# A transformer layer and a gated block on one core: x loaded first, joined sums, other places for small work, and products of ones in three waits

## The reference

```python
p = rms_norm(x, norm_mix) @ w_in                        # 2048 -> all inputs of the two groups
y = concat(rwkv7_group(p_rwkv), dsa_group(p_att))
h = x + y @ w_mix_out
h = h + memory_cross_attention(rms_norm(h, norm_cross), rms_norm(mem, norm_mem), w_q, w_kv, w_o)
h = h + square(relu(rms_norm(h, norm_mlp) @ w_up)) @ w_down
h = rms_norm(h, norm_final)
m = silu(c) @ ada_w + ada_b                             # six rows of 2048
n = rmsnorm(h, norm_g[0]) * (1 + m[1]) + m[0]
z = gelu(n @ a_w_in); u, v = split(z)
h = h + m[2] * ((u * (w_s @ rmsnorm(v, a_g_v) + b_s)) @ a_w_out)
n = rmsnorm(h, norm_g[1]) * (1 + m[4]) + m[3]
g, v = split(dwconv(n @ ffn_w_up))                      # width 3, along the tokens
h = h + m[5] * ((silu(g) * v) @ ffn_w_down)
out = rmsnorm(h, final_g)
```

## Time and profile before

| | us |
|---|---|
| median of 3 runs | 2686.19 (2685.34 to 2686.24) |
| the profiled execution | 2688.38 |
| its span | 2686.5 |
| PE busy | 2634.9 (98%) |
| PEld busy | 2265.3 (84%) |
| DVE busy | 1930.2 (72%) |
| ACT busy | 1388.5 (52%) |
| POOL busy | 128.0 (5%) |
| DMA | 576.28 MB, mean 215 GB/s |

### The profile page before, as it was taken

The page is one execution under the profiler, slowest core; times in us unless marked ns, Lnnn a source line. Parts: engine busy times, 40 slices in busy tenths (PEclk is TensorE's granted clock), DMA queues, the critical chain, the costliest instruction groups (busy, mean ns, idle before and its releaser), DMA issues.

```text
span 2686.5 us, 45958 instructions
## 1 busy us (share of the span) xinstructions
PE 2634.9 (98%) x16884; PEld 2265.3 (84%) x16884; DVE 1930.2 (72%) x2944; ACT 1388.5 (52%) x2156; POOL 128.0 (5%) x142
## 2 busy tenths in 40 slices
PE   9999998999999999999999999999999999999998
PEld 8888887888888888888878888888788888888886
DVE  5677676777787877878887666578777756775675
ACT  5455565666544544535555454445465535553553
POOL 4500001311000000000000000000000000000000
PEclk8999999999999999999999999999999999999999
DMA  6555201655788888887768855588665565556554
GB/s 220 185 180 176 87 4 66 209 193 171 273 291 287 282 296 276 292 285 277 282 241 323 297 181 170 189 271 281 240 196 188 188 196 188 188 193 191 188 188 149
DMA packets 158110, 576.28 MB, mean 215 GB/s; under 512 B 17856, under 2 KB 18400, under 8 KB 157152
## 3 DMA queue, kind: packets, MB, share of 16 engines
q1 hardware_dynamic: 154784, 562.40, 61.6%
q10 hardware_dynamic: 2512, 10.65, 1.1%
q0 software_dynamic: 624, 0.59, 0.1%
HBM read 570.72 MB, written 2.10 MB: 213 GB/s over the span
## 4 chain that ended last, share of the span: by engine, by line
PE 89%; DVE 5%; POOL 3%; ACT 1%; issue 1%; DMA 1%; ACTq 0%; SPq 0%; DVEq 0%; POOLq 0%
PE ps L2566 31%; PE ps L2570 16%; PE ps L2645 12%; PE ps L2646 12%; PE ps L2647 12%; DVE wlo L2170 2%; PE ps L1091 1%; DMA raw<-in_stream 1%; POOL tab L301 1%; PE ps L1731 1%; POOL ssm L1816 1%; POOL tp L302 0%; ACT whi L1836 0%; PE ps L1104 0%; PE ps L2737 0%
## 5 line engine op out<-in xcount | busy, mean ns | idle before, releaser
L2170 DVE TENSOR_TENSOR wlo<-raw,whi 128x1024 fp32r<-128x1024 f32 x872 | 1057.5, 1228 | 540.9 <-ACT whi L1836 537.7
L1836 ACT ACTIVATE whi<-raw 128x1024 fp32r<-128x1024 f32 x872 | 906.0, 1057 | 806.1 <-PE ps L2570 392.1
L2566 PE MATMUL ps<-xn,whi 128*128 128x512 f32 x3760 | 945.0, 393 | 4.4 <-issue 2.0
L2566 PEld LDWEIGHTS ps<-xn,whi 128*128 128x128 f32 x3760 | 676.6, 189 | 126.2 <-issue 3.9
L2570 PEld LDWEIGHTS ps<-xn,wlo 128*128 128x128 f32 x3760 | 511.6, 191 | 37.1
L2570 PE MATMUL ps<-xn,wlo 128*128 128x256 f32 x3760 | 521.2, 282 | 0.0
L2645 PE MATMUL ps<-whi,act_in 128*128 128x512 f32 x1120 | 436.1, 389 | 0.0
L2646 PE MATMUL ps<-wlo,act_in 128*128 128x512 f32 x1120 | 435.8, 389 | 0.0
L2647 PE MATMUL ps<-whi,act_in 128*128 128x512 f32 x1120 | 435.7, 389 | 0.0
L2645 PEld LDWEIGHTS ps<-whi,act_in 128*128 128x128 f32 x1120 | 210.3, 188 | 44.7 <-DVE wlo L2170 1.0
L2647 PEld LDWEIGHTS ps<-whi,act_in 128*128 128x128 f32 x1120 | 210.3, 188 | 43.6
(11 more groups left out here) (336 smaller groups left out, 2226.8 us busy)
## 6 DMA issues: line engine op xcount, KB each, us to landing
raw<-in_stream SPq DMA_DIRECT2D x872, 512.0 KB, 4.2
adaw<-in_ada SPq DMA_DIRECT2D x96, 512.0 KB, 5.7
adaq<-in_ada SPq DMA_DIRECT2D x96, 512.0 KB, 5.3
h<-in_xT SPq DMA_DIRECT2D x4, 512.0 KB, 7.6
memx<-in_memT ACTq DMA_DIRECT2D x1, 2048.0 KB, 9.3
out<-fin SPq DMA_DIRECT2D x4, 512.0 KB, 4.0
lwa<-in_lora ACTq DMA_DIRECT2D x2, 512.0 KB, 5.0
lwa<-in_lora ACTq DMA_DIRECT2D x1, 1024.0 KB, 7.4
```

Of the source, the lines that this page charges most:

```text
L1836: act.activation(whi[:, r, :], raw[:, r, :], ACT.Copy).then_inc(hi_done, 1)
L2170: dve.tensor_tensor(wlo[:, r, :], raw[:, r, :], whi[:, r, :].bitcast(F32), ALU.subtract)\
L2566: return pe.matmul(ps[:, lin.bank(g, t), :], whi[:, (p0 + s) % RING, c * 512 + t * P:c * 512 + (t + 1) * P], x[:, 2 * s + c, :], start=s + ...
```

## The change

1. Beginning. SP issues x alone, in five pieces, waits for the third of them, and then issues ident, slot 0, par, slots 1 to 3 and the masks, all on its own queue. ACT makes 11 squares and DVE 5; DVE adds two squares each, so that PE sums 8 pairs. PE runs products of ones (`warm`) ahead of the sums (12), behind the second, fourth and sixth (3 each), behind the last (5) and behind the spread of the norm's factor (7). DVE makes both halves of chunks 0 and 1 before it splits slot 0.
2. POOL makes tables 2 and 3 first; ACT takes those at step 28, and 0 and 1 at step 36.
3. `spread_k_t` stands at slot 3 of group 10 instead of slot 2, with `key_d`, `decay_sum_d` and `decays_a` one step later. The sum for memory's norm stands at slot 3 instead of 2. In o, all four parts of the activations stand before the split of slot 2. In mlp the norm's sum is cut over slots 4, 5 and 6, and the transposes of h stand one slot later, ACT's copies one step earlier.
4. Token norms. `base_sums` adds three of the four quarters before the last one is there, so the chain has one step less. The last sum of the modulation of the stage (127, 191) stands before the last residual instead of behind the norm's preparation. At g0 and g1 PE runs 13 (10) products of ones when its last group is done and 5 after the root's input is there; chunks 4 to 7 are transposed behind slot 0's products instead of before them in part.
5. End. Six pieces instead of four; the first ones have 512 columns.

The diff, cut to its core (semaphores and one table of counts are left out):

```diff
--- before.py
+++ after.py
@@ -205,7 +205,7 @@
...
-    IA = Steps([sem("index_a")], "s0 s1 s2 s3 rl0 rl1 rl2 rl3 rl4 rl5 rl6 rl7 vt")
+    IA = Steps([sem("index_a")], "s2 s3 s0 s1 rl0 rl1 rl2 rl3 rl4 rl5 rl6 rl7 vt")
@@ -291,7 +291,7 @@
...
-        for q in range(4):
+        for q in (2, 3, 0, 1):
@@ -518,9 +518,9 @@
...
-        if n == 28:
-            act.wait_ge(tab_p, 1 + 4 * 12)
-            for q in range(4):
+        if n in (28, 36):
+            act.wait_ge(tab_p, 1 + 12 * (2 if n == 28 else 4))
+            for q in (2, 3) if n == 28 else (0, 1):
@@ -538,7 +538,7 @@
...
-        if n == 87:
+        if n == 88:
@@ -613,7 +613,7 @@
...
-        if n == 86:
+        if n == 87:
@@ -714,7 +714,7 @@
...
-        if (g, s) == (10, 2):
+        if (g, s) == (10, 3):
@@ -1515,13 +1517,15 @@
...
+    LAST_SUM = {"mlp": ADA_MLP - 1, "a_uo": ADA_MLP + 2 * ADA_V - 1}
+    OUT = [(0, 0, 512, 0), (1, 0, 512, 1), (0, 512, 512, 0), (0, 1024, 1024, 0), (1, 512, 1024, 1), (1, 1536, 512, 0)]
...
-    PIECE_AT = {0: (0, 1), 1: (2,), 5: (3,), 9: (4,)}
+    PIECE_AT = {0: (0, 1), 2: (2,), 5: (3,), 9: (4,)}
@@ -1737,8 +1741,10 @@
...
-        for q in range(4):
-            sp.dma_start(h[:, 4 * q:4 * q + 4, :], A["xT"][:, 4 * q:4 * q + 4, :]).then_inc(x_in[q], 16)
+        for q, (a, b) in enumerate(((0, 4), (4, 8), (8, 12), (12, 14), (14, 16))):
+            sp.dma_start(h[:, a:b, :], A["xT"][:, a:b, :]).then_inc(x_in[q], 16)
+        sp.wait_ge(x_in[2], 16)
+        sp.dma_start(ident[:, :], A["const"][:, C_ID, :]).then_inc(const_in, 16)
@@ -1756,6 +1762,11 @@
...
+        load(0, 0)
+        sp.dma_start(par[:, :], A["par"]).then_inc(par_in, 16)
+        for r in range(1, 4):
+            load(r, r)
+        mixer["loads"](sp)
@@ -1781,11 +1792,10 @@
...
-        for q in range(2):
-            for b in range(2):
-                sp.wait_ge(scaled_d if b == 0 else scaled_a, 10 + q + 1)
-                sp.dma_start(out[b, :, q * 1024:(q + 1) * 1024], fin[:, b, q * 1024:(q + 1) * 1024]).then_inc(out_in, 16)
-        sp.wait_ge(out_in, 64)
+        for k, (b, c, n, e) in enumerate(OUT):
+            sp.wait_ge(scaled_d if e == 0 else scaled_a, 10 + sum(x[3] == e for x in OUT[:k]) + 1)
+            sp.dma_start(out[b, :, c:c + n], fin[:, b, c:c + n]).then_inc(out_in, 16)
+        sp.wait_ge(out_in, 16 * len(OUT))
@@ -1803,7 +1813,7 @@
...
-                pool.sem_inc(ss_done, 1)
+                pool.sem_inc(ss_done, 16)
@@ -1823,9 +1833,6 @@
...
-        act.dma_start(par[:, :], A["par"]).then_inc(par_in, 16)
-        act.dma_start(ident[:, :], A["const"][:, C_ID, :]).then_inc(const_in, 16)
-        mixer["loads"](act)
@@ -1935,12 +1942,20 @@
...
+            buf = (tt, hl)[q % 2]
...
-            squares(h, tt, 0, range(4 * q, 4 * q + 4))
+            if q >= 2:
+                act.wait_ge(xsum_t, 2 * q - 2)
+            for t in (0, 1, 2) if q < 3 else (0, 2):
+                if q == 3 and t == 2:
+                    act.wait_ge(x_in[4], 16)
+                act.activation(buf[:, t, :], h[:, 4 * q + t, :], ACT.Square).then_inc(xsq_a, 1)
+        act.sem_inc(sq_done, 16)
+        norm("mix")
...
-        norm("mix")
+        prepare("mix", chunks=range(2))
...
-        prepare("mix", ahead=split(L["w_in"]))
+        prepare("mix", chunks=range(2, DC), ahead=split(L["w_in"]))
@@ -2024,10 +2039,9 @@
...
-        cross_high(act, 0)
+        for k in range(4):
+            cross_high(act, k)
...
-        for k in range(1, 4):
-            cross_high(act, k)
@@ -2060,7 +2074,7 @@
...
-                if isinstance(i, int) and (i, p) == (0, 8 * k + 17):
+                if isinstance(i, int) and (i, p) == (0, 8 * k + 16):
@@ -2200,6 +2215,8 @@
...
+                last = lambda k: sst[:, k, :, 3]
+                dve.wait_ge(based, {"final": 3, "g1": 5, "out": 7}[nm])
@@ -2214,18 +2231,16 @@
...
-                total = nt[:, 2:2 + n, :]
-                link(dve.tensor_reduce(total, sst[:, 0:n, :, :], AX_X, ALU.add))
-                x = total[:, 0, :]
+                ins = dve.scalar_tensor_tensor(nt[:, 0, :], last(0), -0.5 / D, sbase[:, 0, :], ALU.mult, ALU.add)
...
-            ins = dve.tensor_scalar(half_x if n == 1 else nt[:, 0, :], x, -0.5 / D, -0.5 * eps, ALU.mult, ALU.add)
+                ins = dve.tensor_scalar(half_x, x, -0.5 / D, -0.5 * eps, ALU.mult, ALU.add)
...
-                link(dve.tensor_scalar(nt[:, 6, :], total[:, 1, :], -0.5 / D, None, ALU.mult))
+                link(dve.scalar_tensor_tensor(nt[:, 6, :], last(1), -0.5 / D, sbase[:, 1, :], ALU.mult, ALU.add))
@@ -2239,7 +2254,7 @@
...
-        def prepare(nm, src, gain, shift=None, chunks=range(DC), ahead=None):
+        def prepare(nm, src, gain, shift=None, chunks=range(DC), ahead=None, at_once=False):
@@ -2256,11 +2271,13 @@
...
-                if j:
+                if at_once:
+                    low(j)
+                elif j and (nm != "mix" or j > 2):
...
-            if j == DC - 1:
+            if j == DC - 1 and not at_once:
@@ -2282,7 +2299,9 @@
...
-                if j:
+                if j == 0:
+                    low(0)
+                elif j > 1:
@@ -2300,11 +2319,26 @@
...
+        def base_sums(nm):
+
+            of = HS[nm][1] if nm != "mlp" else "final"
+            n, eps, k = (2, EPS_1, 0) if of == "final" else (1, EPS_2, 3 if of == "g1" else 5)
+            dve.wait_ge(sqt_done, SQT[of] - (4 if of == "final" else 2))
+            dve.tensor_reduce(sbase[:, 0:n, :], sst[:, 0:n, :, 0:3], AX_X, ALU.add).then_inc(based, 1)
+            dve.wait_ge(based, k + 1)
+            dve.tensor_scalar(sbase[:, 0, :], sbase[:, 0, :], -0.5 / D, -0.5 * eps, ALU.mult, ALU.add).then_inc(based, 1)
+            if n == 2:
+                dve.tensor_scalar(sbase[:, 1, :], sbase[:, 1, :], -0.5 / D, None, ALU.mult).then_inc(based, 1)
+
...
+            if sums_h(nm, i) and (q, b) == (3, 0):
+                base_sums(nm)
+                if nm in LAST_SUM:
+                    sum_ada(LAST_SUM[nm])
@@ -2344,11 +2378,27 @@
...
+            buf = (tt, hl)[q % 2]
...
+            for k, t in enumerate((1, 3) if q == 3 else (3,)):
+                if q == 3 and t == 3:
+                    dve.wait_ge(x_in[4], 16)
+                dve.tensor_tensor(buf[:, t, :], h[:, 4 * q + t, :], h[:, 4 * q + t, :], ALU.mult).then_inc(xsq_d, 1)
+                if q == 3:
+                    dve.wait_ge(xsq_d, 4 + k)
+                    dve.wait_ge(xsq_a, 10 + k)
+                    dve.tensor_tensor(buf[:, 2 * k, :], buf[:, 2 * k, :], buf[:, t, :], ALU.add).then_inc(xsum_d, 1)
+            if q < 3:
+                for k in range(2):
+                    dve.wait_ge(xsq_a, 3 * q + 2 + k)
+                    dve.wait_ge(xsq_d, q + 1)
+                    dve.tensor_tensor(buf[:, 2 * k, :], buf[:, 2 * k, :], buf[:, 2 * k + 1, :], ALU.add).then_inc(xsum_d, 1)
+        norm("mix", EPS_1)
...
-        norm("mix", EPS_1)
+        prepare("mix", h, lambda j: col("norm_mix", j), chunks=range(1), at_once=True)
+        prepare("mix", h, lambda j: col("norm_mix", j), chunks=range(1, 2), at_once=True)
...
-        prepare("mix", h, lambda j: col("norm_mix", j), ahead=split(L["w_in"]))
+        prepare("mix", h, lambda j: col("norm_mix", j), chunks=range(2, DC), ahead=split(L["w_in"]))
@@ -2400,10 +2450,9 @@
...
-        cross_low(dve, 0)
+        for k in range(4):
+            cross_low(dve, k)
...
-        for k in range(1, 4):
-            cross_low(dve, k)
@@ -2465,12 +2514,11 @@
...
-        sum_ada(ADA_MLP - 1)
...
-            elif i < 1:
+            elif i == 1:
@@ -2507,7 +2555,6 @@
...
-        sum_ada(ADA_MLP + 2 * ADA_V - 1)
@@ -2677,6 +2725,9 @@
...
+        def turns_before(s):
+            return () if s == 0 else range(4, 8) if s == 1 else (2 * s + 4, 2 * s + 5)
+
@@ -2729,16 +2783,28 @@
...
-        for _ in range(20):
-            pe.matmul(ps[:, stat_bank["mix"] + 2, 0:P], ones[:, :], ones[:, :], start=True, stop=True)
-        for j in range(DC):
-            pe.wait_ge(sq_done, j + 1)
+        def warm(n, bank=stat_bank["mix"] + 2):
+            for _ in range(n):
+                pe.matmul(ps[:, bank, 0:P], ones[:, :], ones[:, :], start=True, stop=True)
+
+        def warm_until(count, lin, before, behind):
+            pe.wait_ge(evac_done, 8 + 4 * (lin.g0 - 1))
+            warm(before, lin.bank(0, 3))
+            pe.wait_ge(rt_done, count)
+            warm(behind, lin.bank(0, 3))
+        warm(12)
+        for k in range(8):
+            pe.wait_ge(xsum_d, k + 1)
+            x = (tt, hl)[k // 2 % 2][:, 2 * (k % 2), :]
...
-                ins = pe.matmul(ps[:, stat_bank["mix"] + c, 0:1], tt[:, j % 4, c * P:(c + 1) * P], ones[:, 0:1],
-                                start=j == 0, stop=j == DC - 1)
-            ins.then_inc(stat_done if j == DC - 1 else ss_done, 1)
+                ins = pe.matmul(ps[:, stat_bank["mix"] + c, 0:1], x[:, c * P:(c + 1) * P], ones[:, 0:1], start=k == 0, stop=k == 7)
```

(21 more changed lines are left out.)

37 lines of the change are left out of this document (22 added, 15 removed).

## The result

| | before | after |
|---|---|---|
| median of 5 runs, us | 2686.19 (2684.93 to 2688.72) | 2670.38 (2666.97 to 2672.16) |
| profiled execution | 2688.38 | 2670.38 |
| its span | 2686.5 | 2668.6 |

The ratio is 0.9938 with a 95% interval of 0.9926 to 0.995: 16.7 us less, 13.4 to 19.9. Forecast were 2667.7, in a range of 2663 to 2677.5, and 18.5 us less. The medians are 15.8 us apart, the two profiled executions 18.0, their spans 17.9. The forecast was made against the profiled execution of before, which was 2.2 us above its median; the one of after is its median.

A forecast was written before the change was run, and what follows sets the result against it. TensorE (PE), busy 98% of the span, was taken as the bound, so only its pauses and slow stretches count. 6.2+6.5+2.6+0.7+2.0+0.5 = 18.5 us off 2688.38 gives 2669.9, lowered by 2.2 to 2667.7; range 2663 to 2677.5.

The forecast's parts named there:

- Beginning: Start of the kernel: x alone first and halved sums bring the first chunks and slots sooner; 6.2 us.
- Then PE sets the pace: Beginning: once x has landed, PE's sums and fills decide when the sum ends, at 11.6 instead of 17.23.
- The bound of 0.6: Beginning: the gain left, 0.6 us, if fills ran at 0.213 and x came at the first 5 us' rate.
- Five places: Tables, spread_k_t, memory norm's sum, o and mlp's transposes: single waits of PE removed; 6.5 us, bounds 0 and 6.5.
- Norm final and g0: Final norm before g0: fills keep the clock and transposes start slots sooner, 2.6 us; SP's stream 0.7; together 3.3.
- g1: Norm at g1: the same as at g0 with 10 and 5 fills; 2.0 us.
- The term for SP: Behind g0: sum 127 made before the norm frees SP's load stream, so two waits for wlo go; 0.7 us.
- End: Writes at the end: one link less (0.2) and a half-size first write issued 0.35 sooner; 0.5 us.
- so the end follows the first issue: End: writes run without a gap at 404 GB/s, so an earlier first issue brings an earlier end.
- The third rival: Slower: PE's clock in the mixer stays at 0.50 longer; 24 us of such work gives 2691.7; chance 0.03.
- Small waits that come back elsewhere: First rival: weights come later than PE wants, so waits return; 12 us gained, 2674.2; chance 0.17.
- Fills that hold the queue: Second rival: products of ones run slowly and delay the transposes at g0 and g1; 5.4 us gained, 2680.8; chance 0.08.

The follow-up runs named there:

- e2: The changed kernel without the three times three products of ones between the sums of squares at the beginning; median 2671.28, ratio 0.9947.
- e12: The kernel of e9 with 14 instead of 12 products of ones at the start, without the three behind the sixth sum; median 2668.16, ratio 0.9936.
- e7: The changed kernel with par, ident and masks on ACT's queue from the start and the slots right behind x; median 2673.22, ratio 0.9955.
- e4: The kernel before with only the products of ones at g0 (13+5) and g1 (10+5) added; median 2682.77, ratio 0.9989.
- e8: The changed kernel with twice the products of ones at g0 (26+10) and g1 (20+10); median 2672.88, ratio 0.9951.
- e1: The changed kernel without the products of ones at g0 and g1; median 2670.51, ratio 0.9946.
- e6: The changed kernel with the old order of transposes and chunks at g0 and g1; median 2667.82, ratio 0.9933.
- e11: The changed kernel with modulation sums 127 and 191 back behind the preparation of g0 and g1; one run, 2671.97.
- e3: The changed kernel with four writes of 1024 columns at the end instead of six; median 2667.53, ratio 0.9933.
- e9: The kernel of e6 with four unequal writes at the end (512, 1024, 1536, 1024 columns); median 2667.23, ratio 0.9932.

## Why the prediction was right, step by step

The mechanisms hold but for two steps, at the beginning (what paces the sums) and at the end. That the sum came so close, 17.9 for 18.5 between the profiles, is partly luck: the five places gave 1.6 us more than forecast, and the beginning, the mixer, g1 and the end 2.2 less. The norm final matches because one of its two terms came out 0.4 too high and the other 0.4 too low.

**Beginning (6.2; measured 5.61).** The times fit (sum ended 12.04 for 11.6, slot 3 at 26.23 for 25.9), but the step "Then PE sets the pace" is wrong. x's landing and DVE's adding pace the sum (the last pair is ready at 11.30, and at 11.14 in e2), and the fills lie in waits, except that the last three delay the end by 0.2 (e12). What they do is keep the clock; without it the sums and fills take twice as long and do stand on the path. e7 shows that x alone on the queue is needed for the gain.

The clock is needed for it too, and there the prediction missed a row. It took the full clock from the window of 5 to 10 us, while in the kernel before the clock is low from 12.5 to 26.2 (and in e4, with the same beginning, from 10.9 to 24.6):

```profile
10.00:15.00 5.00, 5.00 (x37) 5.00 (x36) 0.00 (x0) 3.62 (x10) 0.00 (x0) 0.75 1.02 400
15.00:20.00 5.00, 2.90 (x13) 2.44 (x13) 2.22 (x7) 1.71 (x3) 0.00 (x0) 0.50 0.42 166
```

After, both windows show 1.00. Where the clock falls in the new beginning as well (e8), 1.55 us of the 5.61 are left; 0.7 of the loss is that x came later there (last pair at 12.01), the other 3.4 come with the clock low. So more than half of this gain stands only as long as the clock does. The bound of 0.6, meant for slow fills and a slow x, allowed for this, but as one unknown for the kernel and not as something that differs from one execution to the next.

**Five places (6.5; 8.1).** All five gained, and none of the waits came back as a wait. None was undone in a run of its own; each is read from the place at which the two traces part. The sizes were off, mlp's most (3.04 for 1.9). Before, the last product ahead of the first lot of transposes starts at 691.87 and the next one behind them at 694.64; without the 0.23 of the product itself that is 2.54 us for the wait and 16 transposes. After, without a wait, it is 685.49 to 687.27, less 0.12: 1.66. The idle time of that wait is 0.66 us (the 0.7 of the earlier trace rows), and 0.88 went: a stop of PE costs some 0.2 more than its idle time. 0.16 of it is that the last product is counted as busy for 0.39 us where its successor would have followed in 0.23. The same with o (1.58 for 1.33), spread_k (1.06 for 0.80) and the tables (1.57 for 1.40). mlp has four such stops, so 0.8 to 0.9 of its 1.1; the rest is open. Memory's norm gave 0.25 us less than its wait.

By the rows the tables' edit did more than its own 1.57: it let the beginning's gain through. POOL ends the last table at 101.36 before and at 98.52 after, 2.8 us sooner, while PE is 5.6 us ahead. With the old order ACT would still wait for all four. e4, which has the old order, shows what comes of that: its profile is 0.71 us ahead at 112.46 and has nothing left of it at the next product (115.08, before 114.97), since the wait has grown from 1.4 to 2.2:

```profile
PE ps L2566 <- DVE wi L590: 2.2, 1, 2.2
```

From the end of the last table (101.36 before, 101.48 in e4) to that product it is 13.6 us both times. An estimate from this: with the old order the changed kernel's would start near 112.1 and not at 107.79, 4.3 us later. No run has the new beginning with the old tables.

**Norm final and g0 (3.3; 3.3), g1 (2.0; 1.7).** The fills fitted, with 0.2 us to spare, and the clock stayed. But the forecast gave the gain to three edits that don't add up: the fills alone give 4.2 (e4), on top of the rest 1.8 (e1), and the order of transposes, counted as "1.5 earlier", costs 0.95 with the clock full (e6). The order does bring the first wide product 0.5 us sooner (8.56 us into g0's stretch, 9.09 in e6), as it was meant to, but slot 1, which counts, comes later. The term for SP was 0.7 and is 1.14, more in e11. So the 3.3 is 2.2 and 1.1 where 2.6 and 0.7 were forecast.

**End (0.5; −0.27).** The failed steps are "so the end follows the first issue" and "Two more issues are hidden behind the writes". The issue did come 0.47 sooner, as forecast, but from there to the end six writes take 0.74 us longer than four. The rows of the issues on SP (shortest, median and longest in ns, then the start of the first and the last), before and after:

```profile
L1787 SPq DMA_DIRECT2D out<-fin x4: 353/608/1192, 2679.6 to 2681.3; - x4
...
L1797 SPq DMA_DIRECT2D out<-fin x6: 353/444/1202, 2660.9 to 2663.4; - x6
```

The end comes 5.2 us after the start of the *last* issue in both, and that starts 1.71 us after the first before and 2.46 after: the 0.75. The pieces are not late: ACT and DVE have scaled the last at 2662.15 and 2662.33, and SP, whose six issues follow one another without a pause, comes to the last write at 2663.37. With four writes the issues span 1.70 us again (e3, 1.69 in e9), and the end is 5.24 and 5.35 behind the last. Whether an issue takes its time by itself or is held up by the writes ahead of it (the last one takes 1.2 us in both) is open. The smaller packets are a small part at most: 160 ns for 4 KB and 84 for 2 KB in the trace, 0.13 us for the lot.

**The mixer (0; −0.48).** The third rival feared a longer stretch at 1.2 GHz here. In these two profiles there is one, at a fiftieth of the 24 us that it needed. The two windows are of the same work, 8 us apart; the clock is 0.83 and 1.00 before, 0.73 and 0.76 after:

```profile
448.00:458.00 10.00, 7.10 (x47) 5.67 (x45) 7.64 (x26) 5.12 (x14) 5.97 (x8) 0.83 0.16 46
458.00:468.00 10.00, 6.48 (x36) 5.20 (x36) 6.47 (x21) 8.31 (x27) 6.00 (x8) 1.00 0.90 375
```

```profile
440.00:450.00 10.00, 7.88 (x47) 6.31 (x45) 7.54 (x26) 5.02 (x14) 5.96 (x8) 0.73 0.15 43
450.00:460.00 10.00, 7.88 (x35) 6.29 (x35) 6.49 (x21) 8.48 (x28) 6.00 (x8) 0.76 0.92 376
```

PE is busy 2.5 us more (182.5 for 180.0) and the stage is 0.48 longer, because most of it fits in its waits. That the change is the cause is not shown. The stretch (271 to 468 before) takes 193.7 to 197.5 us in the fourteen profiles, and the time at 1.2 GHz in it goes from 3.4 to 17.1: at most 6.8 us in the six shortest (193.7 to 195.8), 10.2 to 13.7 in the next five, 17.1 in the three longest (197.4 to 197.5). The kernel before has 10.2 (and e4 13.7), the changed kernel 17.1, and e3 and e11, which have the same list of work up to there, 6.8 and 10.2. These differences, and those of the beginning, are as large as the 2 to 5 us by which runs of one kernel scatter; what decides them in an execution stays open.

**The rivals.** Small waits that come back elsewhere: 0.25 us at one place. Fills that hold the queue: not at the norms, where they had 0.2 us to spare; at the beginning they do when the clock falls (e2, e8).

## What to carry to other kernels

A product of ones in a wait is worth what the clock gives to the work that PE is late with, which the low stretch alone does not tell: taking the 18 and 15 products out of the changed kernel cost 1.6 us at one norm (low for 6.8 us) and 0.2 at the other (3.4 us), while putting them into the kernel before gained 2.1 at each. Size them to end just ahead of the awaited work, since beyond it each costs its full 0.22 us. Price a reordering again once the clock is kept: the new order of transposes cost 0.95 us there, although without the fills the rest of the change gained 2.1 at the same two norms. When a stage is made faster, ask what else has to be ready by its own time: by the estimate above the tables would have held up most of what the beginning gained. And the end followed the last issue of the writes here, not the first, so two more pieces cost more than the earlier first piece gained.

## What the runs showed that I had not expected

Two profiles with the same beginning differ by 4.1 us, with the clock full in one and at 1.2 GHz from 8.9 to 19.2 us in the other, though PE's list is the same there and PE rested less ahead of the fall (0.32 against 0.79 us in front of the first sum). The third piece of x came 0.7 us later in the one that fell; whether that has to do with it was not tried. And stretches outside of the beginning and the mixer repeat to 0.01 to 0.05 us (g0's is 13.42 to 13.45 in five profiles with the same code there), so that an edit of 0.2 us can be read from one profile where medians of five runs can't tell 2. At the beginning it can't: there full-clock profiles of the same code differ by 0.76 us.
